# Norms of keys, queries and outputs in a gated DeltaNet kernel: from column sums and diagonals to one product with ones and a power by logarithm and exponential

## The reference, cut to what matters

```python
def l2norm(x):
    return x * lax.rsqrt(jnp.sum(x * x, axis=-1, keepdims=True) + EPS)
...
    q = l2norm(q.astype(f32)) * (dk ** -0.5)
    k = l2norm(k.astype(f32))
...
        o = gated_delta_rule(q, k, v, g, beta)
        o = rms_norm(o, dn_out_norm[i]) * jax.nn.silu(dn_z.reshape(b, s, DN_HEADS, DN_HEAD_DIM))
```

## Time and profile before

| | |
|---|---|
| median of 3 runs | 1885.56 us (1884.22 to 1886.51) |
| the profiled execution | 1886.01 us, span in the trace 1884.1 us |
| PE busy | 1833.6 us, 97% |
| DVE busy | 1200.9 us, 64% |
| ACT busy | 899.1 us, 48% |
| POOL busy | 255.8 us, 14% |
| mean granted PE clock | 0.989 |

### The profile page before, as it was taken

The page is one execution under the profiler, slowest core; times in us unless marked ns, Lnnn a source line. Parts: engine busy times, 40 slices in busy tenths (PEclk is TensorE's granted clock), DMA queues, the critical chain, the costliest instruction groups (busy, mean ns, idle before and its releaser), DMA issues.

```text
span 1884.1 us, 30329 instructions
## 1 busy us (share of the span) xinstructions
PE 1833.6 (97%) x10842; PEld 1603.2 (85%) x10842; DVE 1200.9 (64%) x1412; ACT 899.1 (48%) x1034; POOL 255.8 (14%) x371
## 2 busy tenths in 40 slices
PE   7889999999999999999999999999999999999996
PEld 5778888888888888888888888888888888888885
DVE  5776767967846656665666666555655555555576
ACT  5554444444546545545444544444444444434453
POOL 4051230610510000000011000000000000000044
PEclk9999999999999999999999999999999999999998
DMA  6345453453555556555555555555555556565552
GB/s 223 112 144 157 128 168 119 156 161 112 173 176 167 173 174 200 189 183 195 171 193 197 189 179 187 190 193 186 178 193 193 190 170 205 176 202 180 188 179 101
DMA packets 103100, 327.40 MB, mean 174 GB/s; under 512 B 23088, under 2 KB 23216, under 8 KB 103024
## 3 DMA queue, kind: packets, MB, share of 16 engines
q1 hardware_dynamic: 89024, 321.43, 51.9%
q10 hardware_dynamic: 13632, 3.67, 0.9%
q0 software_dynamic: 368, 1.31, 0.2%
HBM read 323.23 MB, written 3.15 MB: 173 GB/s over the span
## 4 chain that ended last, share of the span: by engine, by line
PE 90%; DVE 4%; issue 2%; ACT 2%; POOL 1%; DVEq 0%; DMA 0%; ACTq 0%; SPq 0%; POOLq 0%
PE acc L282 54%; PE acc L287 28%; DVE wlo L275 1%; PE ps L594 1%; PE ps L600 1%; PE acc L303 1%; PE acc L304 1%; PE acc L305 1%; POOL sqsum L445 1%; ACT whi L267 0%; PE ps L658 0%; PE ps L560 0%; ACT ax L956 0%; DVE pre L1312 0%; PE ps L626 0%
## 5 line engine op out<-in xcount | busy, mean ns | idle before, releaser
L275 DVE TENSOR_TENSOR wlo<-raw,whi 128x1024 fp32r<-128x1024 f32 x604 | 756.2, 1270 | 449.0 <-ACT whi L267 440.7
L282 PE MATMUL acc<-ax,whi 128*128 128x512 f32 x3328 | 846.7, 396 | 10.4 <-ACT whi L267 10.4
L267 ACT ACTIVATE whi<-raw 128x1024 fp32r<-128x1024 f32 x604 | 624.7, 1054 | 476.8 <-PE acc L287 444.8
L282 PEld LDWEIGHTS acc<-ax,whi 128*128 128x128 f32 x3328 | 602.6, 190 | 123.6 <-issue 13.9
L287 PEld LDWEIGHTS acc<-ax,wlo 128*128 128x128 f32 x3328 | 456.5, 191 | 33.6 <-DVE wlo L275 0.5
L287 PE MATMUL acc<-ax,wlo 128*128 128x256 f32 x3328 | 466.1, 283 | 0.0
L282 PE MATMUL acc<-fx,whi 128*128 128x512 f32 x704 | 176.3, 392 | 0.0
L282 PEld LDWEIGHTS acc<-fx,whi 128*128 128x128 f32 x704 | 126.6, 189 | 22.6
L503 POOL TENSOR_TENSOR sqsum<-sqsum,t 128x512 f32<-128x512 f32 x16 | 22.1, 1379 | 706.5 <-ACT t L1211 706.5
L921 ACT ACTIVATE t<-acc 128x512 f32<-128x512 f32 x88 | 52.5, 596 | 131.5 <-PE acc L287 131.5
L1312 DVE TENSOR_TENSOR t<-acc,t 128x512 f32<-128x512 f32 x88 | 60.8, 691 | 81.0 <-ACT t L921 80.6
(11 more groups left out here) (247 smaller groups left out, 1357.4 us busy)
## 6 DMA issues: line engine op xcount, KB each, us to landing
raw<-in_win SPq DMA_DIRECT2D x224, 512.0 KB, 3.5
raw<-in_wgu SPq DMA_DIRECT2D x176, 512.0 KB, 4.4
raw<-in_wd SPq DMA_DIRECT2D x88, 512.0 KB, 4.3
raw<-in_wb SPq DMA_DIRECT2D x32, 512.0 KB, 4.4
raw<-in_wo SPq DMA_DIRECT2D x32, 512.0 KB, 4.5
raw<-in_wpg SPq DMA_DIRECT2D x32, 512.0 KB, 4.1
raw<-in_wa SPq DMA_DIRECT2D x16, 512.0 KB, 4.9
xT<-in_xT SPq DMA_DIRECT2D x4, 512.0 KB, 8.0
```

Source lines behind the costliest of these rows:

```text
L267: nc.scalar.activation(whi[:, s], raw[:, s], ACT.Copy).then_inc(hi_done, 1)
L275: nc.vector.tensor_tensor(wlo[:, s], raw[:, s], whi[:, s].bitcast(F32), ALU.subtract).then_inc(lo_done, 1)
L282: nc.tensor.matmul(o, whi[:, s, kt, m * P:(m + 1) * P], x[:, k].rearrange("p q n -> p (q n)"), start=begin, stop=False, skip_group_check=True)
```

## The change

The column sums, the reciprocals, the roots of 8 columns and the diagonals go. PE's `rows` now takes the squares themselves: ones times squares puts the sum over features on all partitions. ACT reads the 128 x 1024 sums from `ps[0]`, takes the logarithm with the epsilon as bias, and then the exponential of -0.5 times it, both 128 x 1024; `norm_k` and `norm_o` read that result from `t[1]` and `t[2]`. The squares of q are scaled by 128 * 128 * EPS as they are made and added to those of o by a new DVE function `o_add`. `k_root` moves from step 12 to 13 of ACT's `START` table (13 to 14 in `FIRST`), `norm_k` from 13 to 14 on DVE, `gram_m`, `make_negm`, `store_m`, `load_m`, `transpose_k` and `scale_k` each one step later, `o_rt` from 14 to 22 and `norm_o` from 15 to 24.

```diff
@@ PE @@
-            def k_columns(g):
-
+            def k_rows(g):
                 pe.wait_ge(qk_sq, 2 * g + 1)
-                columns(t[1], 1, qk_len)
-
-            def k_rows(g):
-                pe.wait_ge(k_diag_done, g + 1)
+                if isinstance(g, int):
+                    pe.wait_ge(rcol_done, 1)
                 rows(t[1], k_rows_out)
...
-            def q_columns(g):
-                pe.wait_ge(qk_sq, 2 * g + 2)
-
-                pe.wait_ge(ps_free, g + 1)
-                columns(t[0], 0, qk_len)
...
-            def o_columns(d):
-
-                pe.wait_ge(delta_act, 3 * d + 3)
...
             def o_row(d):
-                pe.wait_ge(o_diag, d + 1)
+                pe.wait_ge(o_added, d + 1)
+                pe.wait_ge(norm_logged, 2 * d + (1 if isinstance(d, int) else 2))
                 rows(t[2], o_rows)
...
-            START = {1: g_rows, 11: k_columns, 12: k_rows, 14: gram_m, 17: transpose_k, 21: q_gram_columns, 26: transpose_v}
+            START = {1: g_rows, 12: k_rows, 15: gram_m, 18: transpose_k, 21: gram_q, 26: transpose_v}
@@ ACT @@
-                f(t[c][:], conv[c][:], ACT.Square).then_inc(qk_sq, 1)
+                if c == 0 and not isinstance(g, int):
+                    act.wait_ge(o_added, g)
+                f(t[c][:], conv[c][:], ACT.Square, scale=1.0 if c else P * EPS ** 0.5).then_inc(qk_sq, 1)
...
-            def k_root(d):
-                act.wait_ge(k_inv, d + 1)
-                f(length[:, 1], length[:, 1], ACT.Sqrt).then_inc(k_rooted, 1)
+            def k_root(g):
+                act.wait_ge(k_rows_out, g + 1)
+                f(t[1][:], psv[0], ACT.Ln, bias=epsc[:, 0:1]).then_inc(norm_logged, 1)
+                act.wait_ge(norm_logged, 1 if isinstance(g, int) else 2 * g)
+                f(t[1][:], t[1][:], ACT.Exp, scale=-0.5).then_inc(k_root_made, 1)
...
             def o_rt(d):
-                act.wait_ge(o_mean, 2 * d + 2)
-                f(length[:, 2], length[:, 2], ACT.Sqrt).then_inc(o_root, 1)
+
+                act.wait_ge(o_rows, d + 1)
+                f(t[2][:], psv[0], ACT.Ln, scale=1.0 / P, bias=epsc[:, 1:2]).then_inc(norm_logged, 1)
+                act.wait_ge(norm_logged, 2 * d + (2 if isinstance(d, int) else 3))
+                f(t[2][:], t[2][:], ACT.Exp, scale=-0.5).then_inc(o_root_made, 1)
@@ DVE @@
-            def diagonal(c, signal):
-
-                v.tensor_tensor(t[c][:].rearrange("p h (m n) -> p (h m) n", n=P), over(ident[:], 8), bc(length[:, c], P),
-                                ALU.mult).then_inc(signal, 1)
...
             def norm_k(g):
-                dve.wait_ge(k_rows_out, g + 1)
-                v.tensor_tensor(kn[:], psv[0], conv[1][:], ALU.mult).then_inc(k_normed, 1)
+                dve.wait_ge(k_root_made, g + 1)
+                v.tensor_tensor(kn[:], t[1][:], conv[1][:], ALU.mult).then_inc(k_normed, 1)
...
+            def o_add(d):
+
+                dve.wait_ge(delta_act, 3 * d + 3)
+                dve.wait_ge(qk_sq, 2 * d + 2)
+                v.tensor_tensor(t[2][:], t[2][:], t[0][:], ALU.add).then_inc(o_added, 1)
...
             def norm_o(d):
 
                 dve.wait_ge(o_gained, d + 1)
-                dve.wait_ge(o_rows, d + 1)
+                dve.wait_ge(o_root_made, d + 1)
                 o = oT[:, ds(GROUP * d, GROUP)]
-                v.tensor_tensor(o, o, psv[0], ALU.mult).then_inc(ps_free, 1)
+                v.tensor_tensor(o, o, t[2][:], ALU.mult).then_inc(ps_free, 1)
```

More of the change, by code:

```diff
@@ L587, in tok_tile @@
                 return ap[:, h, m * P:(m + 1) * P]
[L589 to L595, removed]
             def rows(src, signal):
@@ L753, in outputs @@
                 last.then_inc(delta_out, 1)
-            def o_columns(d):
-                pe.wait_ge(delta_act, 3 * d + 3)
-                if not isinstance(d, int):
-                    pe.wait_ge(k_normed, d + 2)
-                columns(t[2], 2, o_len)
             def o_row(d):
-                pe.wait_ge(o_diag, d + 1)
+                pe.wait_ge(o_added, d + 1)
+                pe.wait_ge(norm_logged, 2 * d + (1 if isinstance(d, int) else 2))
                 rows(t[2], o_rows)
             FINISH = {5: merge32_a, 6: merge32_b, 7: merge64_a, 8: merge64_b, 9: first_tile, 10: carry,
-                      11: second_tile, 12: outputs, 13: o_columns, 14: o_row}
-            FIRST = {12: k_columns, 13: k_rows, 16: g_rows, 17: gram_m, 19: transpose_k, 22: q_gram_columns, 26: transpose_v}
-            START = {1: g_rows, 11: k_columns, 12: k_rows, 14: gram_m, 17: transpose_k, 21: q_gram_columns, 26: transpose_v}
+                      11: second_tile, 12: outputs, 14: o_row}
+            FIRST = {13: k_rows, 16: g_rows, 17: gram_m, 20: transpose_k, 22: gram_q, 26: transpose_v}
+            START = {1: g_rows, 12: k_rows, 15: gram_m, 18: transpose_k, 21: gram_q, 26: transpose_v}
             def stages(d, g, n0, width):
@@ L1072, in _ @@
             FINISH = {1: (silu_z1,), 2: (store_x,), 3: (load_diag,), 6: (copy_p32,), 7: (copy_inv,), 10: (copy_v0,), 12: (copy_v1,),
-                      13: (square_o,), 14: (o_rt,)}
-            FIRST = {11: (silu_k,), 13: (k_root,), 17: (g_copy,), 18: (decay_m,), 20: (store_m,), 21: (load_m, silu_q),
+                      13: (square_o,), 22: (o_rt,)}
+            FIRST = {11: (silu_k,), 14: (k_root,), 17: (g_copy,), 18: (decay_m,), 20: (store_m,), 21: (load_m, silu_q),
                      23: (g_exp, decay_q), 25: (silu_v,), 29: (silu_z0,)}
-            START = {2: (g_copy,), 10: (silu_k,), 11: (decay_m,), 12: (k_root,), 15: (store_m,), 16: (load_m,), 18: (silu_q,),
+            START = {2: (g_copy,), 10: (silu_k,), 11: (decay_m,), 13: (k_root,), 16: (store_m,), 17: (load_m,), 18: (silu_q,),
                      20: (g_exp, decay_q), 25: (silu_v,), 29: (silu_z0,)}
@@ L1489, in _ @@
             FINISH = {5: (turn_diag,), 7: (copy_invT32,), 8: (copy_p64,),
-                      9: (copy_invT64,), 10: (copy_nwT,), 11: (copy_state,), 13: (o_gain,), 14: (o_inv, o_diagonal), 15: (norm_o,)}
-            FIRST = {11: (select_heads,), 13: (k_mean, k_diag), 14: (norm_k,), 18: (diff_m,), 19: (make_negm,), 21: (scale_k, diff_q),
-                     23: (q_mean,), 25: (make_qkT,), 26: (decay_q,), 27: (scale_v,)}
-            START = {0: (select_heads,), 10: (diff_m,), 12: (k_mean, k_diag), 13: (norm_k,), 15: (make_negm,), 17: (diff_q,),
-                     18: (scale_k,), 22: (q_mean, decay_q), 25: (make_qkT,), 27: (scale_v,)}
+                      9: (copy_invT64,), 10: (copy_nwT,), 11: (copy_state,), 14: (o_add, o_gain), 24: (norm_o,)}
+            FIRST = {11: (select_heads,), 15: (norm_k,), 18: (diff_m,), 19: (make_negm,), 21: (scale_k, diff_q),
+                     25: (make_qkT,), 26: (decay_q,), 27: (scale_v,)}
+            START = {0: (select_heads,), 10: (diff_m,), 14: (norm_k,), 16: (make_negm,), 17: (diff_q,),
+                     19: (scale_k,), 22: (decay_q,), 25: (make_qkT,), 27: (scale_v,)}
             FIRST_CONV = {8: conv_a(1, 0), 9: conv_b(1, 0), 15: conv_a(0, 1), 17: conv_b(0, 1), 22: conv_a(2, 2), 24: conv_b(2, 2)}
```

45 lines of the change are left out of this document (12 added, 33 removed).

## The result

| | before | after |
|---|---|---|
| median | 1885.76 us (1884.22 to 1886.51) | 1894.34 us (1892.91 to 1895.88, 5 runs) |
| profiled execution, span | 1886.01, 1884.1 us | 1892.91, 1891.0 us |
| mean granted PE clock | 0.989 | 0.983 |

The ratio is 1.0046, with a 95% interval of 1.0033 to 1.006: slower, 8.6 us by the medians and 6.9 by the profiled executions. 1896 had been forecast.

The account below looks back on a forecast made before the run. PE, busy 97% of the span, was taken to bound the kernel. Group 0 -4.8, groups 1 to 3 +4.3, last group -0.7 and clock +11.9 gave +10.7 us on 1886.0, so 1896, range 1875 to 1902.

Parts of the forecast that it names:

- What goes: On PE: removed `columns` calls 20.4, a wait 6.4 and a cold stretch 1.8, 28.6 us if nothing else moved.
- What comes on ACT: Each norm costs load, logarithm, load, exponential: 1.28 a load, 1.06 a pass, 4.7 us a norm.
- o_row: Groups 1 to 3: PE waits 3.4 us, giving back both removed calls; last group waits 1.0 of 1.70 saved.
- transpose_v: Groups 1 to 3: PE waits 4.5 us for make_qkT; each group ends 1.4 us later, +4.3 us.
- Group 0: g_rows idles 4.9 us; transpose_v waits 3.65 and starts at 124.6 instead of 129.44: -4.8 us.
- The clock: Half clock behind waits: 7.9 at three transpose_v, 2.7 at o_row, 1.3 in group 0; +11.9, bounds 0 and 16.
- The sum: Whole kernel: work and waits -1.2, clock +11.9, together +10.7 us on the profiled 1886.0; 1896 taken.
- Same: Waits as computed, clock stays up at most of them: one or two falls, 1885 to 1889; chance 0.17.
- Faster: Chain from k_root to make_negm and make_qkT about 1 us shorter at each of two waits: 1878; chance 0.20.
- One load in a pair: Norms without the second load: o_row waits 2.1, transpose_v 3.2, fewer falls, 1884 to 1888; chance 0.02.

Follow-up runs that it names:

- root_27: Changed kernel with o_rt (ACT) and norm_o (DVE) at step 27 in groups 1 to 3 instead of 22 and 24; 1888.34 us.
- norm_late_tv: Changed kernel with o_add and o_gain at step 13, transpose_v at 27, scale_v at 28, norm_o at 28 in groups 1 to 3; 1859.14 us.
- root_late: Changed kernel with o_rt at step 28 of ACT and norm_o at 29 of DVE in groups 1 to 3; 1897.9 us.
- no_log: Changed kernel with an identity of the same size in place of the logarithm; 1885.73 us.
- filler: Changed kernel with eight products that nobody reads added on PE ahead of transpose_v in all four groups; 1885.09 us.
- all_27: Changed kernel with o_add, o_gain at 13, o_rt, norm_o at 27 (groups 1 to 3), and in group 0 k_root at 15, norm_k at 16; 1874.65 us.
- before_tv: Kernel before with transpose_v at step 27 instead of 26 and scale_v at 28 instead of 27; 1878.19 us.
- after_tv: Changed kernel with transpose_v at step 27 instead of 26 and scale_v at 28 instead of 27; 1871.88 us.
- both_27: Changed kernel with o_add and o_gain at step 13, and o_rt and norm_o at 27 in groups 1 to 3; 1874.1 us.
- both_tv: Changed kernel with o_add, o_gain at 13, transpose_v at 27, scale_v at 28, and in groups 1 to 3 o_rt at 26, norm_o at 28; 1871.31 us.
- add_early_tv: Changed kernel with o_add and o_gain at step 13, transpose_v at 27 and scale_v at 28; 1865.8 us.

## Why the prediction was right, step by step

**What goes.** Right: no row of `columns` is left, and `k_rows` of group 0 has no wait.

**What comes on ACT.** 1.06 was taken for each pass; the logarithm took 1.12, the exponential 1.06, each load 1.28, 4.74 us a norm instead of 4.7. By the Trainium skill (ScalarE: Activation LUTs, Table sets: the hidden batching unit) logarithm and exponential share a set and take one load. The trace after has a load ahead of each in all eight norms, so in this program the measurement decides against the rule. The Trainium skill (ScalarE: Activation LUTs, What ACT_TABLE_LOAD costs) gives 1283 ns for the load itself and some 1380 ns of drain with it, 2.66 us for a switch. The trace agrees with the first, 1.28 us each, and shows nothing of the second: the logarithm starts 1.30 us behind the start of its load, the exponential too. Whether the program could be made to keep the shared set was not tried.

**`o_row`.** 3.4 us in each of three groups and 1.0 in the last were forecast, 3.11 and 0.89 came. From `o_row` to `transpose_v` the time grew from 42.83 us to 46.02, of which 1.7 is a fall of the clock; the forecast had 44.3 without it.

**`transpose_v`.** 4.5 forecast, 4.45, 4.39 and 4.43 measured. The chain named (`make_negm`, the stores and loads on ACT, the splits, `norm_o` in the row) is what the trace shows, and root_27 and norm_late_tv moved the wait by moving its links. One sum in it is off: ACT's pieces add up to 232.4, not 232.0, for the split of step 21. The trace has that split where the forecast put it, 25.0 us behind `o_row` once the 1.7 of the fall are taken off, as 232.0 - 206.95.

**Group 0.** `transpose_v` 3.65 forecast, 3.19 measured; a gain of 4.8 forecast, 5.4 measured (7.7 less the 2.3 of the start). `g_rows` 4.9 forecast, 4.55 measured. A step was missing, though it cost nothing: the clock also fell behind `g_rows`. From 78.34 to the low part of its half at 85.62 are 7.28 us, where norm_late_tv, warm in group 2, takes 3.87. PE is held by `make_negm` at `transpose_k` anyway: in root_late the stretch behind `g_rows` is 0.95 us shorter, `transpose_k` waits 1.06, and it starts 35.73 us behind `k_rows`, as in the changed kernel, where it was to wait 1.4 and did not. In no_log, where the call of `g_rows` took 1.99, it waited 2.7.

**The clock.** The sum had +11.9: 7.9 for three falls at `transpose_v`, half prices for the others. Measured, a fall there costs 6.04 - 3.70 = 2.34 in group 1 and 2.38 and 2.42 in the next, instead of 2.62, 7.1 in all; in group 0, 5.32 - 3.70 = 1.6 instead of 1.3; behind `o_row` 6.22 - 4.52 = 1.7 in group 1, and almost nothing in groups 2 and 3, where the call took 1.98 and 1.99 us, against 2.7 forecast for the three. That is 10.4, and filler measured 9 for those at `transpose_v` alone. One more fall came where the forecast, going by the earlier trace rows, had none: behind `merge64_b`, after the same wait of 2.23 us. First the kernel before, where `merge64_b` starts at 541.36, then the kernel after:

```profile
545.25 1.05 PE L724 MATMUL ps<-vbeta,invT 128*128 128x128 f32 x8
...
547.34 1.11 PE L696 MATMUL ps<-p,inv 64*64 64x64 f32 x16 [2.23 <-DVE p L1405]
...
548.90 0.63 PE L302 MATMUL acc<-wlo,ax 128*128 128x512 f32 x1
...
552.84 1.05 PE L703 MATMUL ps<-vbeta,invT 128*128 128x128 f32 x8
```

`merge64_b` itself kept its 1.11, but the products behind it took 0.63 us and not 0.39 or 0.40, and the stretch took 5.50 us instead of 3.89: 1.6 more, 12.0 in all.

**The sum, and its luck.** Without the falls of the clock, group 0 gained 5.4 (4.8 forecast), groups 1 to 3 lost 3.2 (4.3 forecast) and the rest gained 0.7, as forecast: -2.9 instead of -1.2. The clock took 12.0 instead of 11.9, and that agreement is luck, since its four parts were off by -0.8, +0.3, -1.0 and +1.6. So the change cost 9.1 us where 10.7 had been forecast, and the start, which the change does not touch, gave 2.3 back: +6.9 in the profiled execution, +8.6 in the medians. The waits and their chain were foreseen; that 1896 lies within 2 us of 1894.34 is finer than the forecast could know.

**The rivals.** *Same* fails: the clock stayed up at none of the four `transpose_v`. *Faster* fails: the waits were as long as forecast. *One load in a pair* had 1884 to 1888; no_log, with no load at all, took 1885.73, but its `transpose_v` waits did not shrink to 3.2 as that rival said; they stayed at 4.4 to 4.6.

## What to carry to other kernels

Work taken off the busy engine is worth nothing at a place where it then stands and waits: walk each queue from the new work to the next wait, and count the fall of the clock behind the wait as part of its price (here 21.9 us more at two waits, 12 of falls and some smaller new waits outweighed a saving of 28.6). Then look for the cheap cure, which is often to move the one that waits: `transpose_v` a half later gave 22.5 us, while moving the root on ACT and `norm_o` cost 3.6 (root_late) or gave 6.0 (root_27), because the splits behind it then came late. Before a difference between two schedules is put down to a wait, add up the falls of the clock in both traces: in root_late and all_27 they were larger than the change of the waits. In a queue that also feeds others, a function has free places and dear ones a step or two apart, and a table load that it forces on the next function counts with it.

## What the hardware showed unexpectedly

**The length of an idle stretch did not decide by itself whether the clock fell.** `merge64_b` waits 2.23 us in all fourteen kernels here. From its start to the product behind its half are 3.9 us in three of them (the kernel before, before_tv, after_tv), 5.4 to 5.5 in seven and 6.9 to 7.0 in four (root_27, both_27, both_tv, norm_late_tv). `transpose_v` ran warm after 1.65 us in after_tv and cold after 2.22, 2.18 and 2.09 in add_early_tv. After 3.11 us of waiting the stretch from `o_row` to `gram_m` took 4.6 us in two groups of the changed kernel and 7.3 to 7.4 in the same two of root_late. Behind `g_rows` (products with only 16 rows, 1.99 us) the clock fell after a wait of 0.83 us in the kernel before and not after one of 0.88 in norm_late_tv: the first products of the half behind took 2.92 us in the one and 2.12 in the other. What besides the wait decides is open. Such a place costs between nothing and some 3 us, which a forecast can bound but not fix.

**Products for nothing made the kernel faster.** Some 3.6 us of PE work, four times, gave 9.3 us.
